# The first two tiles of the output projection, issued between the steps that fold the paged attention

## The reference, cut to what is touched

```python
def mla_sample(q_nope, q_rope, new_rows, cache_l, page_table, lp):
    past = cache_l[page_table].reshape(Bd, -1, KV_CACHE_DIM)
...
    p = jax.nn.softmax(s, axis=-1).astype(new_rows.dtype)
    n_past = past.shape[1]
    ctx = jnp.einsum('bhtk,bkc->bthc', p[..., :n_past], pc) + jnp.einsum('bhtk,bkc->bthc', p[..., n_past:], nc)
    o = jnp.einsum('bthc,chd->bthd', ctx, lp["w_uv"])
...
def mixer_out(attn, rec, lp):
    return jnp.concatenate([attn, rec], axis=-1) @ lp["w_out"]
...
        xp = xp + mixer_out(attn, rec, lp)
...
        xs = xs + mixer_out(attn, rec, lp)
```

## Time and profile before

| | before |
|---|---|
| median of three runs | 1049.38 us |
| the profiled execution, its own time | 1052.64 us |
| span of the profiled execution | 1050.5 us |
| TensorE busy | 1001.0 us, 95% of the span |
| VectorE, ScalarE, GpSimd busy | 515.1, 299.6, 442.7 us |
| share of TensorE in the chain that ended last | 81% |
| granted TensorE clock, mean | 0.99 of full speed |

### The profile page before, as it was taken

The page is one execution under the profiler, slowest core; times in us unless marked ns, Lnnn a source line. Parts: engine busy times, 40 slices in busy tenths (PEclk is TensorE's granted clock), DMA queues, the critical chain, the costliest instruction groups (busy, mean ns, idle before and its releaser), DMA issues.

```text
span 1050.5 us, 19847 instructions
## 1 busy us (share of the span) xinstructions
PE 1001.0 (95%) x8532; PEld 903.9 (86%) x8532; DVE 515.1 (49%) x730; ACT 299.6 (29%) x611; POOL 442.7 (42%) x282
## 2 busy tenths in 40 slices
PE   4999989979999999899999899999999999999997
PEld 4989987756777777799975599999999999999996
DVE  3889986568465555365145356541242134114413
ACT  5333266357334443111034212210010012002212
POOL 3445567600001112265520055555655655655651
PEclk9999999999899999999999999999999999999999
DMA  7423355520657773733185023223223223223222
GB/s 186 118 65 81 84 150 137 146 91 31 238 204 271 272 271 132 247 95 91 51 309 211 2 67 95 80 81 99 83 82 100 82 83 99 81 83 99 82 81 85
DMA packets 144013, 129.84 MB, mean 124 GB/s; under 512 B 13093, under 2 KB 136882, under 8 KB 140086
## 3 DMA queue, kind: packets, MB, share of 16 engines
q1 hardware_dynamic: 138344, 87.99, 28.4%
q0 software_dynamic: 2304, 37.75, 9.3%
q10 hardware_dynamic: 3278, 2.83, 0.8%
HBM read 123.53 MB, written 5.03 MB: 122 GB/s over the span
## 4 chain that ended last, share of the span: by engine, by line
PE 81%; DVE 11%; ACT 3%; issue 2%; DMA 2%; POOL 1%; ACTq 1%; DVEq 0%; POOLq 0%
PE gps L534 56%; PE gps L850 5%; PE aux L864 3%; PE aux L891 2%; PE aux L806 1%; PE gps L982 1%; PE gps L1057 1%; PE aux L870 1%; DMA wraw<-in_w_mem_v_dram 1%; DVE q L1776 1%; PE gps L828 1%; POOL wlo L476 1%; PE aux L995 1%; PE aux L1016 1%; PE aux L881 1%
## 5 line engine op out<-in xcount | busy, mean ns | idle before, releaser
L534 PE MATMUL gps<-act_hi,whi 128*128 128x272 f32 x944 | 275.0, 291 | 5.3 <-DVE act_lo L1552 2.8
L534 PE MATMUL gps<-act_lo,whi 128*128 128x272 f32 x944 | 274.1, 290 | 0.0
L463 POOL TENSOR_SCALAR whi<-wraw 128x1024 fp32r<-128x1024 f32 (+1 forms) x110 | 114.4, 1040 | 378.4 <-PE gps L534 321.4
L534 PE MATMUL gps<-act_hi,wlo 128*128 128x272 f32 x944 | 273.7, 290 | 0.0
L466 POOL TENSOR_TENSOR wlo<-wraw,whi 128x1024 fp32r<-128x1024 f32 (+1 forms) x110 | 260.7, 2370 | 9.2
L534 PE MATMUL gps<-h_hi,whi 128*128 128x272 f32 x640 | 185.7, 290 | 0.0
L534 PE MATMUL gps<-h_lo,whi 128*128 128x272 f32 x640 | 185.0, 289 | 0.0
L534 PE MATMUL gps<-h_hi,wlo 128*128 128x272 f32 x640 | 184.6, 288 | 0.0
L534 PEld LDWEIGHTS gps<-act_hi,whi 128*128 128x128 f32 x944 | 179.1, 190 | 5.8 <-issue 4.0
L534 PEld LDWEIGHTS gps<-act_hi,wlo 128*128 128x128 f32 x944 | 179.0, 190 | 0.0
L534 PEld LDWEIGHTS gps<-act_lo,whi 128*128 128x128 f32 x944 | 178.8, 189 | 0.0
(11 more groups left out here) (352 smaller groups left out, 1466.2 us busy)
## 6 DMA issues: line engine op xcount, KB each, us to landing
wraw<-in_w_up_dram SPq DMA_DIRECT2D x32, 512.0 KB, 4.1
wraw<-in_w_down_dram SPq DMA_DIRECT2D x32, 512.0 KB, 4.0
wraw<-in_w_in_dram SPq DMA_DIRECT2D x14, 512.0 KB, 3.9
kv<-in_cache_mem_k_dram SPq DMA_DIRECT2D x7, 1024.0 KB, 7.1
kv<-in_cache_mem_v_dram SPq DMA_DIRECT2D x7, 1024.0 KB, 13.3
wraw<-in_w_mem_k_dram SPq DMA_DIRECT2D x8, 512.0 KB, 4.0
wraw<-in_w_mem_v_dram SPq DMA_DIRECT2D x8, 512.0 KB, 4.0
wraw<-in_w_out_dram SPq DMA_DIRECT2D x8, 512.0 KB, 4.2
```

Of the source, the lines that this page charges most:

```text
L463: nc.gpsimd.tensor_scalar(whi[:, slot, 0:n], wraw[:, slot, 0:n], 1.0, 1.0, ALU.mult, ALU.mult).then_inc(pool_step, 1)
L534: mm = nc.tensor.matmul(out_of(a), w_of(w, k), x_of(x, k, part), start=(k == 0 and s == 0), stop=(k == k_tiles - 1 and s == 2))
```

## The change

The 96 matmuls of tiles 0 and 1 are taken out of `act_tile` and issued in pieces by `out_part(i, a, ks)`: tile i, column half a, input blocks ks, three matmuls for each block. Nothing else is computed, and no matmul is added or dropped. The six waits that stood behind the fold, and those of `act_tile`, go ahead of the first piece. The accumulation of tile 0 and tile 1 now begins with block 4. In `gps` all four banks are in use by the two tiles during the fold, so the fold's transposes go to bank 0 of `aux` and the products with `w_uv` to bank 3 of `aux`. The order on PE is now:

| step of the fold | piece behind it (matmuls) |
|---|---|
| maxima and sums (L915, L918) | tile 0, first half, blocks 4, 5 (6) |
| `values` of the last chunk | tile 0, first half, 6, 7 (6); tile 0, second half, 4, 5 (6) |
| spreading of the weights | tile 0, second half, 6, 7 (6); tile 0, first half, 0, 1 (6) |
| sums over the chunks | tile 0, first half, 2 (3) |
| transposes of group 0 | tile 0, first half, 3 (3) |
| transposes of group 1 | tile 1, first half, 4 to 7 (12) |
| products with `w_uv` | tile 1, second half, 4 to 7 (12) |
| wait for `so_lo` | tile 0, second half, 0 to 3 (12): tile 0 done; tile 1, first, 0 to 3 (12); tile 1, second, 0 to 3 (12): tile 1 done |

Sixty matmuls stand ahead of the wait for `so_lo` and 36 behind it. Tiles 2 to 7 are as before.

```diff
+            def out_part(i, a, ks):
+                for k in ks:
+                    for s, (w, x) in enumerate(((0, 0), (1, 0), (0, 1))):
+                        mm = nc.tensor.matmul(gps[:, 2 * i + a, 0:HALF], weights(i, 128, w, k, 0, 128),
+                                              (act_hi, act_lo)[x][:, k, T_PARTS[a]],
+                                              start=(k == 4 and s == 0), stop=(k == 3 and s == 2))
+                return mm
+
+            pe.wait_ge(gl_lo, NW)
+            pe.wait_ge(at_lo, 4)
+            pe.wait_ge(g_td, 4 * NH)
+            pe.wait_ge(g_ta, 4 * NH)
+            pe.wait_ge(tile_free[0], T_OUT // 2)
+            pe.wait_ge(tile_free[1], T_OUT // 2)
+            pe.wait_ge(w_ready, U_OUT + 1)
+            out_part(0, 0, (4, 5))
             values(NH - 1)
+            out_part(0, 0, (6, 7))
+            out_part(0, 1, (4, 5))
             pe.wait_ge(fold_dve, 2)
...
+            out_part(0, 1, (6, 7))
+            out_part(0, 0, (0, 1))
             pe.wait_ge(fold_dve, 3)
...
             for g in range(2):
+                out_part(0, 0, (g + 2,))
                 pe.wait_ge(fold_dve, g + 4)
                 for c in range(2):
-                    mm = nc.tensor.transpose(gps[:, 0, 256 * c + 128 * g:256 * c + 128 * g + 128],
+                    mm = nc.tensor.transpose(aux[:, 0, 256 * c + 128 * g:256 * c + 128 * g + 128],
...
+            pe.wait_ge(w_ready, U_OUT + 2)
+            out_part(1, 0, (4, 5, 6, 7))
...
-                    mm = nc.tensor.matmul(aux[r:r + 64, 0, TS * (h // 2):TS * (h // 2) + TS],
+                    mm = nc.tensor.matmul(aux[r:r + 64, 3, TS * (h // 2):TS * (h // 2) + TS],
...
-            pe.wait_ge(gl_lo, NW)
-            pe.wait_ge(at_lo, 4)
+            out_part(1, 1, (4, 5, 6, 7))
             pe.wait_ge(so_lo, 1)
-            pe.wait_ge(g_td, 4 * NH)
-            pe.wait_ge(g_ta, 4 * NH)
-            for i in range(8):
+            out_part(0, 1, (0, 1, 2, 3)).then_inc(tile_done, 1)
+            out_part(1, 0, (0, 1, 2, 3))
+            out_part(1, 1, (0, 1, 2, 3)).then_inc(tile_done, 1)
+            for i in range(2, 8):
                 act_tile(U_OUT + i, T_OUT + i)
```

More of the change, by code:

```diff
@@ L1440, in _ @@
             act.wait_ge(so_ps, 1)
-            nc.scalar.copy(act_hi[:, 0:4, TP:T], aux[:, 0, 0:4 * TS].rearrange("p (k n) -> p k n", k=4)
+            nc.scalar.copy(act_hi[:, 0:4, TP:T], aux[:, 3, 0:4 * TS].rearrange("p (k n) -> p k n", k=4)
                            ).then_inc(so_hi, 1)
@@ L1886, in _ @@
             dve.wait_ge(fold_pe, 5)
-            V.tensor_copy(ctxa[:, :, :, :].rearrange("p c b q -> p (c b q)"), gps[:, 0, :]).then_inc(fold_dve, 1)
+            V.tensor_copy(ctxa[:, :, :, :].rearrange("p c b q -> p (c b q)"), aux[:, 0, :]).then_inc(fold_dve, 1)
             dve.wait_ge(so_hi, 1)
-            V.tensor_tensor(act_lo[:, 0:4, TP:T], aux[:, 0, 0:4 * TS].rearrange("p (k n) -> p k n", k=4),
+            V.tensor_tensor(act_lo[:, 0:4, TP:T], aux[:, 3, 0:4 * TS].rearrange("p (k n) -> p k n", k=4),
                             act_hi[:, 0:4, TP:T].bitcast(F32), ALU.subtract).then_inc(so_lo, 1)
```

## The result

The changed kernel took 1044.8 us as the median of six runs (1043.74 to 1049.08), against 1050.88 us for six runs of the kernel before beside it. The ratio is 0.994, with a 95% interval of 0.9919 to 0.996. The forecast of -0.43% lies in both intervals. The profiled execution took 1049.08 us with a span of 1046.8 us.

What follows compares the result with a forecast made beforehand. TensorE, idle in pieces within the fold and at a low clock behind it, was taken as the bound. Tile 2 starting at 438.90 instead of 443.44 us gives 4.5 us: 1049.38 - 4.5 = 1044.9 us, range 1043.0 to 1047.6.

Steps and rivals of the forecast that it cites:

- the mark: First matmul of tile 2, where what can be won ends: 443.44 us before, 438.90 us forecast.
- given back: Rival: the gain is lost again behind tile 7, 0 us, 1049.4; chance 0.04 together with the change not working.
- The walk: Step-by-step times through the fold in the new order: `values` 0.96 us later, sums 2.3, L952 3.06, tile 2 at 438.90.
- The seven waits: Waits ahead of the first piece, in front of `values`: 0 to 0.6 us, taken as 0.3 us.
- The switch itself: TensorE going from narrow to full-width matmuls in the fold: 0.35 us each; all nine switches taken as 1.7 us.
- The rival in which neither costs anything: No price for waits and switches in the fold: -6.0 us, 1043.4; chance 0.12.
- The new bound: Ahead of tile 2: GpSimd's split of unit 2 must wait for tile 0, so TensorE stands 0.9 us.
- The clock: Pieces fill the idle time, so every matmul runs at full clock; the low stretch before lost 1.4 us.
- the slower rival: Clock low within the fold, each piece delaying the chain at double length: +5.8 us, 1055.2; chance 0.03.
- The moved transfers: Loads issued later: unit 3 lands 8.5 us after issue, split with 0.5 us of cover ahead of tile 3; nothing lost.
- The rival that this load comes late: Unit 3 lands 12 us after its issue, TensorE stands 3.0 us: gain only 1.5 us, 1047.9; chance 0.07.
- The median: Median time of the whole kernel: 1049.38 - 4.5 = 1044.9 us, 0.43% less.

Runs made afterwards that it cites:

- the 60 pieces as dead weight: Changed kernel with all 60 early matmuls' results thrown away and tiles 0 and 1 made in full behind the fold; ratio 1.0013.
- the filled gaps: Against the changed kernel: only 27 throw-away matmuls in the fold's gaps, tiles 0 and 1 made in full behind it; ratio 0.9989.
- The last experiment: Changed kernel with three memory-cache blocks (3 MB) queued ahead of unit 3 instead of one; 635.29 us from the last score reduction to the end.
- the second set: The changed kernel timed again without change, nine runs; median 1048.84 us against 1052.23 us for the kernel before, ratio 0.9965.
- the second profile without pieces in the first half: Repeat profile of the changed kernel with the 30 matmuls ahead of the sums moved behind the products with `w_uv`; fold 29.22 us, ratio 0.9969.

## Why the prediction was right, point by point

**What bounds it, and the mark.** Right: 4.4 us at tile 2, 4.3 us at the end. The gain isn't given back.

**The walk.** From the start of the last L881, forecast and measured in the changed kernel: `values` 2.40 and 2.14 us; the spreading 5.85 and 5.71; the sums 7.78 and 7.64; group 1's transposes 10.61 and 10.63; L952 (now L977) 12.45 and 12.45; tile 2 20.55 and 20.55. The last figures are closer than the terms deserve: two small errors cancel. The seven waits cost nothing there: the first piece starts 1.18 us after L881, as soon as the short matmuls have drained, and not 1.55. Up to L977 the same 0.37 us is lost again, about 0.1 us at each of the four pieces that follow narrow matmuls: the first matmul of such a piece holds the array 0.23 us (428.54 to 428.77 us in the timeline) where I had counted 0.127. The two pieces behind the full-width transposes lose nothing of the kind: from 429.02 to 429.37 us two transposes and the first matmul of a piece take 0.35 us, no more than 2 x 0.11 + 0.127. The switch itself was right, 1.87 us from a `values` of 32 loads to the next full-width matmul for 1.84. With the 60 pieces as dead weight L977 is late by 3.06 us as well, the forecast's own figure.

The Trainium skill's page "Advanced Engine Details and Errata" (Network/Comms) gives 50 to 100 ns for each read of a semaphore; by my estimate seven at that price would have put the first piece at 1.6 us or later, which the trace doesn't bear out. Uncovered, in the kernel with the filled gaps, the seven cost at most 0.18 us together.

The rival in which neither costs anything (-6.0 us) is out.

**The new bound.** Right: the split of unit 2 stood between tile 0 and tile 2, 0.74 us of TensorE's idle time by the profile for a forecast of 0.9, and moving six matmuls took nearly all of it away.

**The clock.** Right in its effect: 1.00 through the fold in all seven profiles in which it was filled from its start, 0.50 for some 3 us in both profiles of the kernel before. The forecast's 1.4 us is the upper end of the 0.9 to 1.4 us that the filled gaps bought. Seven of seven against three of four is what says that filling the fold takes the low stretch away; with the same program once low and once not, no single profile proves it. The transfers don't decide it: over 426 to 430 us of the changed kernel they kept their engines at 0.97 of their time, and the clock was 1.00. The prediction's argument that the clock had stayed 1.00 through the whole fold, given against the slower rival, doesn't hold: in two of the four sparse profiles it fell during the sums.

The Trainium skill's page "TensorE: Matmul & The Clock Gate" (Why this matters for your kernels) says that idle gaps between bursts cost the clock. I had read it against the forecast. The last experiment agrees with it plainly (3.91 us idle, then 0.50), and the filled gaps agree in direction, though no single gap of the fold was over some 1 us. Idle time isn't the whole of it: a low stretch between 260 and 285 us, where the earlier trace rows count TensorE as busy throughout, is in all eleven profiles, and I didn't test what brings it. How often a sparse fold meets a low stretch is open.

**The moved transfers.** The direction was right and the size was off to the safe side. Unit 3 was issued at 433.0 us and landed 6.3 us later, not 8.5, and its split was over at 443.5 us, 2.2 us ahead of tile 3 and not 0.5. The rival that this load comes late didn't happen; the last experiment shows it is real. For a landing 12 us after the issue I had 3.0 us; at 11.4 us the hold was 4.1 us, because the issue too came later, and the low clock behind it cost 1.6 us more.

**The median.** Forecast 1044.9, measured 1044.8 us: partly luck. The kernel before had a median of 1050.88 us in that comparison and not 1049.38, so the measured difference was 6.1 us there, and 3.4 us in the second set; the fold accounts for 4.4 us. Two executions of the kernel before, taken side by side for its second profile, took 1048.71 and 1054.04 us. What moves whole executions by up to 5 us ahead of the fold I didn't test. It isn't the low clock there alone: by stretches of 5 us it lasted some 20 us ahead of 410 us in the second profile without pieces in the first half and some 10 us in the last experiment's, and both reached the reduction within 0.06 us of each other (415.75 and 415.81 us).

## What to carry to other kernels

Where a chain passes between engines in short steps, work that is ready can stand in TensorE's gaps even if each piece is a little longer than its gap: 60 early matmuls pushed the chain by 3.1 us and saved 7.6 us of later work. Add up TensorE's own time, with 0.35 us for each switch from narrow to full width and 0.1 us for the first matmul behind it, and look at once for what was covered by the work you moved: here the next weights' split, which wanted tile 0 to end early, and a shared load queue, where 2 MB more ahead of a weight unit cost 5.7 us, 1.6 of it because the clock fell behind the long wait. Where executions vary by more than the change, measure from a point that both programs reach alike.

## What the runs showed of the hardware

- A granted clock of 0.50 for about 3 us came in three of four profiles with a sparse fold, at no fixed step, and in none of seven with a filled one. The same program had it in one execution and not in the next (fold of 30.91 and 29.22 us). Throw-away matmuls in the gaps shortened the fold by 0.6 to 1.1 us.
- Behind 3.91 us of idle TensorE the clock fell to 0.50 about half a microsecond after the engine had resumed, and cost 1.6 us over the next 19 matmuls.
- Seven fulfilled waits cost TensorE nothing while short matmuls were queued ahead of them, and at most 0.18 us together when it stood idle.
- After a switch from narrow matmuls to full width the first matmul of a piece held the array 0.23 us, the next ones 0.127 us, so such a piece cost 0.1 us beside the switch. A piece behind full-width transposes didn't (0.35 us for two transposes and its first matmul).
- A 512 KB weight load issued behind one 1 MB block of a busy queue landed after 6.3 us, behind 3 MB after 11.4 us.
